# Summing the first layer's modulation on VectorE, and spreading the key lengths from a 128x8 tile

## The chip, the cores and the metric

The kernel runs on one core of one Trainium2 chip. The metric is device time in microseconds; runs of the kernel before are given as a median of three. It is one program with five instruction streams (TensorE for products, VectorE and ScalarE for elementwise work, POOL and SP for issuing transfers), each strictly in the order in which it is written, tied together by semaphores.

## The reference, cut to what matters

The model is a hybrid layer (a recurrent branch with eight heads and a dilated attention, then a mixture of experts) and behind it two further layers, each steered by a modulation vector. Two places matter here. The modulation of both later layers depends only on a conditioning vector `c` and can be computed at any time before its layer:

```
c_act = silu(c)                              # 1 x 1024
for l in range(2):
    mod = c_act @ w_ada[l] + b_ada[l]        # 1024 x 6144 weights (24 MB) for 6144 numbers
    sh_m, sc_m, gt_m, sh_f, sc_f, gt_f = split(mod, 6)
```

The keys of the recurrent branch are divided by their length in each head of 64 channels:

```
kk = heads(k * k_k)
kk = kk / maximum(sqrt(sum(kk * kk, axis=-1)), 1e-12)
wkv = scan(S = S * w + (S @ -kk) (kk * a)^T + v k^T, y = S @ r), both directions, added
```

There are 512 tokens, 1024 channels, and 8 heads of 64 channels in the recurrent branch.

## The kernel before, in words

**Stages.** A front (to 143 us) normalizes x and computes the columns of the recurrent branch. The recurrence follows (143 to 641 us), then the dilated attention, the mixture of experts, and the two later layers. The change touches the front and the recurrence; in the last layer's modulation it renames buffers.

**The recurrence** works on one pair of heads at a time, channels of both heads on the 128 partitions, 512 tokens on the free axis: four rounds, `pr` 0 to 3. Both directions `d` of the scan are done side by side. A round has a *preparation*, steps i = 5 to 28 (8 to 28 in round 0, whose first steps stand in the front), and a *row loop* of 8 chunks. `recurrence_order` (line 655) is one list of steps that all engines walk through, each doing its own part of a step. In each preparation step TensorE does 16 products of 64x64x64 (32 passes) for d = 0 and again for d = 1 (`rw_prep`, line 938) into bank 4 and bank 5, and another engine evicts each bank: ScalarE for steps 5 to 7 (line 1506), VectorE for the others (line 1994). Steps 8 to 12 make masked products (`MASKS`; step 12 gives two tiles, Dt and Lt), step 13 makes R0 from Dt on VectorE, and steps 14 to 28 are the chain `PRODS` (line 416): Dt2, D2, R0a, D4, R1a, R1b, R1c, QT, GT, Ha, Hb, KV, Hc, U1, W1T. Each of them needs the eviction of an earlier one, mostly the one ahead of it; step 14 waits for R0. There is a single bank for each direction, so an eviction also frees the bank for the next step.

**Woven work.** Between the steps stand other things, so that TensorE has something to do while a bank is evicted: in 19 of 24 steps one bank of a large product of the next stages (`rw_gemm`, line 1020), whose weights are split by ScalarE into halfH and by VectorE into halfL when a new tile begins (`split_to`, lines 1421 and 1833); the norming of the round before (`rw_norming`, VectorE); sums, scales, gains and rotations of the attention's heads (VectorE), and turns of them (TensorE into bank 6, ScalarE out of it); and the two pieces that the change is about.

**The modulation before.** `ada()` in `recurrence_order` (line 673) spreads 54 steps `("ada", g, k)` over the rounds: 9, 18, 18 and 9. In a step with k < 8 TensorE multiplies a tile of 128x1024 weights by one column of `cact` (`rw_ada`, line 1044): four products of 256 columns that write one row each. POOL loads these tiles, 48 of 512 KB, into two buffers `ada0` and `ada1`; the one for step n is issued when TensorE has done step n - 2. At k = 7 ScalarE copies the four rows to `arow`, and at k = 8 TensorE turns them (two products) and VectorE copies them to `mods`. The last layer is done otherwise, beside the feed-forward product of the layer ahead of it: VectorE multiplies a 128x1024 tile by the column and adds it to `m_acc`, transposes in blocks of 32 and reduces after eight tiles, and TensorE adds the four parts up at the end (`modulation`, lines 1066 and 2611).

**The key lengths before.** `rw_kk`: VectorE multiplies by k_k and squares; TensorE multiplies the squares by a block matrix of ones, so that each length stands on all 64 partitions of its head (128x512, line 915); ScalarE takes the root (line 1477); VectorE takes the maximum with 1e-12, the reciprocal of 128x512 and the product (line 1929). The four steps stand in four successive preparation steps of the round before (i = 5 to 8, in round 0 8 to 11), and for round 0 in the front.

**The end of the recurrence.** After the last woven tile (in step 28 of round 3) SP issues the transfers of the queries and keys for the attention (`sync_program`, line 2828). The bonus of each round (`rw_bonus`, lines 968 and 2019) stands between its preparation and its loop: VectorE forms rk2 when both W1T are evicted, TensorE multiplies it by one column.

## Time and profile before

| | |
|---|---|
| median of 3 runs | 3043.69 us (3041.87 to 3046.1) |
| the profiled execution | 3046.71 us, span 3044.8 us |
| TensorE busy | 2824.5 us, 93% |
| VectorE busy | 1586.8 us, 52% |
| ScalarE busy | 898.4 us, 30% |
| POOL busy | 109.2 us, 4% |
| chain that ended last | TensorE 78%, VectorE 12%, ScalarE 5%, DMA 2% |

The span is what the profile covers; the device time has some two microseconds around it. A matmul's end is modelled, so that two rows of TensorE may overlap: the distance of their starts is what a thing costs. An fp32 product appears as two instructions (passes). "Idle before" is the idle time of the engine ahead of an instruction, with what ended it.

### The profile page before, as it was taken

What the parts mean: (1) busy time and instruction counts of PE and PEld (TensorE: products, weight loads), DVE (VectorE), ACT (ScalarE), POOL (GpSimd) and SP (SyncE); (2) the same over time, 40 slices, a digit from 0 to 9 for tenths busy, and PEclk for the clock granted to TensorE, in tenths of its full rate; (3) what the DMA queues carried; (4) which work ended last, traced back from release to release, by engine and by line L of the source; (5) the groups of instructions that cost most, each with busy time, mean ns of one, the idle gap of its engine ahead of it and who ended that gap; (6) DMA issues with size and microseconds to landing.
All of it is one profiled execution on the core that took longest, in us unless ns stands there. A gap on an engine that the chain in (4) does not pass through costs nothing.

```text
span 3044.8 us, 47336 instructions
## 1 busy us (share of the span) xinstructions
PE 2824.5 (93%) x20508; PEld 2037.3 (67%) x20508; DVE 1586.8 (52%) x2926; ACT 898.4 (30%) x1449; POOL 109.2 (4%) x187
## 2 busy tenths in 40 slices
PE   7999999989979999989988999999999889999999
PEld 5777777866723333338666677888786656878887
DVE  4656565655543333345665456666456664554343
ACT  5323222225300100022333533223323335333131
POOL 0000000000000000000000000000000000000000
PEclk9999999999989999999998999999999989999999
DMA  4224233251399999953242334564232333323322
GB/s 146 84 75 136 85 112 119 71 188 74 104 393 427 427 426 427 427 224 93 66 97 70 131 98 151 188 198 151 83 88 70 103 71 107 102 80 93 101 94 83
DMA packets 148822, 476.87 MB, mean 157 GB/s; under 512 B 12816, under 2 KB 40064, under 8 KB 136192
## 3 DMA queue, kind: packets, MB, share of 16 engines
q1 hardware_dynamic: 114400, 367.62, 33.3%
q0 software_dynamic: 24128, 87.81, 8.8%
q10 hardware_dynamic: 10080, 18.35, 2.1%
q8 instruction: 163, 2.67, 0.4%
q14 instruction: 51, 0.42, 0.1%
HBM read 452.23 MB, written 21.51 MB: 156 GB/s over the span
## 4 chain that ended last, share of the span: by engine, by line
PE 78%; DVE 12%; ACT 5%; DMA 2%; issue 2%; POOL 0%; DVEq 0%; ACTq 0%; SPq 0%; POOLq 0%
PE psum L156 75%; PE psum L159 3%; DVE halfL L165 2%; DVE sc__234 L195 2%; DVE m L192 1%; ACT halfH L162 1%; DVE X L165 1%; DMA kT<-qk_rows 1%; DVE a20S L180 1%; DVE a21S L180 1%; DVE n_ht L168 1%; ACT a1S L162 1%; DVE slot L165 0%; DVE slot L186 0%; ACT a21S L162 0%
## 5 line engine op out<-in xcount | busy, mean ns | idle before, releaser
L165 DVE TENSOR_TENSOR halfL<-ring,halfH 128x1024 fp32r<-128x1024 f32 x302 | 368.2, 1221 | 605.2 <-ACT halfH L162 604.4
L162 ACT ACTIVATE halfH<-ring 128x1024 fp32r<-128x1024 f32 x302 | 317.1, 1053 | 747.9 <-PE psum L156 739.4
L156 PE MATMUL psum<-hH,halfH 128*128 128x512 f32 x1200 | 492.0, 410 | 9.0 <-DVE hL L165 5.3
L156 PE MATMUL psum<-hL,halfH 128*128 128x512 f32 x1200 | 476.3, 397 | 0.0
L156 PE MATMUL psum<-hH,halfL 128*128 128x512 f32 x1200 | 475.6, 396 | 0.0
L156 PEld LDWEIGHTS psum<-hH,halfH 128*128 128x128 f32 x1200 | 230.5, 192 | 90.8 <-issue 35.1
L156 PEld LDWEIGHTS psum<-hH,halfL 128*128 128x128 f32 x1200 | 230.4, 192 | 50.6
L156 PEld LDWEIGHTS psum<-hL,halfH 128*128 128x128 f32 x1200 | 231.2, 193 | 44.4 <-issue 0.2
L156 PE MATMUL psum<-halfH,hH 128*128 128x512 f32 (+2 forms) x576 | 225.8, 392 | 25.8 <-DVE hL L165 12.2
L156 PE MATMUL psum<-wslot,XT 128*64 128x512 f32 x1024 | 247.3, 606 | 0.8 <-DVE XT L165 0.8
L156 PE MATMUL psum<-halfH,hL 128*128 128x512 f32 (+2 forms) x576 | 214.8, 373 | 0.0
L156 PE MATMUL psum<-halfL,hH 128*128 128x512 f32 (+2 forms) x576 | 214.7, 373 | 0.0
L165 DVE TENSOR_TENSOR X<-X,psum 128x512 f32<-128x512 f32 x136 | 93.2, 687 | 215.8 <-PE psum L156 212.6
L156 PEld LDWEIGHTS psum<-halfH,hH 128*128 128x128 f32 x576 | 115.0, 200 | 56.3 <-issue 29.5
L156 PEld LDWEIGHTS psum<-wslot,XT 128*64 128x64 f32 x1024 | 64.3, 137 | 126.6 <-issue 125.4
L156 PEld LDWEIGHTS psum<-slot,slot 64*64 64x64 f32 x4096 | 124.6, 135 | 24.9 <-issue 18.1
L156 PE MATMUL psum<-halfH,aH 128*128 128x512 f32 x352 | 136.9, 389 | 0.0
L156 PE MATMUL psum<-halfL,aH 128*128 128x512 f32 x352 | 136.9, 389 | 0.0
L156 PE MATMUL psum<-halfH,aL 128*128 128x512 f32 x352 | 136.9, 389 | 0.0
L156 PE MATMUL psum<-slot,slot 64*64 64x64 f32 x4096 | 133.3, 220 | 3.9 <-DVE slot L165 1.9
L156 PEld LDWEIGHTS psum<-halfH,hL 128*128 128x128 f32 x576 | 115.1, 200 | 17.8
L156 PEld LDWEIGHTS psum<-halfL,hH 128*128 128x128 f32 x576 | 115.6, 201 | 14.8
(456 smaller groups left out, 4140.7 us busy)
## 6 DMA issues: line engine op xcount, KB each, us to landing
wslot<-in_w_gate SPq DMA_DIRECT2D x32, 2048.0 KB, 18.4
wslot<-in_w_up SPq DMA_DIRECT2D x32, 2048.0 KB, 18.9
wslot<-in_w_down SPq DMA_DIRECT2D x32, 2048.0 KB, 19.5
ring<-in_w_in SPq DMA_DIRECT2D x120, 512.0 KB, 3.7
ring<-in_w_gu SPq DMA_DIRECT2D x88, 512.0 KB, 3.5
ada<-in_w_ada POOLq DMA_DIRECT2D x48, 512.0 KB, 4.2
m_in<-in_w_ada POOLq DMA_DIRECT2D x48, 512.0 KB, 4.8
ring<-in_w_down SPq DMA_DIRECT2D x44, 512.0 KB, 3.9
```

Of the source, the lines that this page charges most:

```text
L156: return self.e.matmul(*a, **k)
L159: return self.e.transpose(*a, **k)
L162: return self.e.activation(*a, **k)
L165: return self.e.tensor_tensor(*a, **k)
L168: return self.e.tensor_scalar(*a, **k)
L180: return self.e.tensor_tensor_reduce(*a, **k)
L192: return self.e.max(*a, **k)
L195: return self.e.match_replace(*a, **k)
```

## The change

1. **Modulation of the first later layer.** The `ada` steps of TensorE and ScalarE, `arow` and the 48 tiles of 128x1024 go. VectorE does what it did for the last layer, on 96 tiles of 128x512: one at each preparation step (two at steps 16, 20 and 24 of round 0), none in the loops. After eight tiles it transposes and reduces. Both layers share one function on VectorE, POOL and TensorE, with widths 512 and 1024. TensorE's closing products stand in the loop of round 3, chunk 2, and VectorE's copy to `mods` at chunk 4. POOL issues 96 transfers of 256 KB.
2. **Key lengths.** TensorE sums into 128x8 (a token in each partition, tile and head in the columns), ScalarE's root and VectorE's maximum and reciprocal work on 128x8, and TensorE spreads the result over the head's 64 partitions with eight products against the identity (a fifth step, `spread`), from whose bank VectorE multiplies.
3. **Evictions.** QT, KV, U1 and W1T are evicted by ScalarE (`BY_ACT`) instead of VectorE.

```diff
+    BY_ACT = ("QT", "KV", "U1", "W1T")
+    m_in0, m_acc0, m_turn0 = [rk(f"m_in0{i}", 512) for i in range(2)], rk("m_acc0", 512), rk("m_turn0", 512)
+    MODULATION = [(m_in0, m_acc0, m_turn0, 512), (m_in1, m_acc1, m_turn1, 1024)]
...
-                 (2, 3): early("kds") + [("U", 2), ("shift", 0)] + early("Kt"),
+                 (2, 3): [("kk", 0, "spread")] + early("kds") + [("U", 2), ("shift", 0)] + early("Kt"),
...
-                if pr < 3 and i < i0 + 4:
-                    yield "kk", pr + 1, ("squares", "sums", "root", "inverse")[i - i0]
+                if pr < 3 and i < i0 + 5:
+                    yield "kk", pr + 1, ("squares", "sums", "root", "inverse", "spread")[i - i0]
...
-                for _ in range(2 if i in ((6, 7) if pr else (8, 9, 10, 11, 12)) else 1):
-                    yield from ada()
+                for _ in range(2 if not pr and i in (16, 20, 24) else 1):
+                    yield "ada",
...
+                if pr == 3 and s in (2, 4):
+                    yield ("mods", "mods_out")[s // 2 - 1],
...
# TensorE, rw_kk
-                pe.matmul(bank(Y_BANK), K("blk"), SL[0]["t1"], start=True, stop=True).then_inc(*up("rw_pe", "kk_sum", pr))
+                for t in range(4):
+                    i = pe.matmul(bank(Y_BANK)[:, 2 * t:2 * t + 2], SL[0]["t1"][:, t * 128:(t + 1) * 128],
+                                  K("blk")[:, 0:128:64], start=True, stop=True)
+                i.then_inc(*up("rw_pe", "kk_sum", pr))
                 free[Y_BANK] = [("kk_sqrt", pr)]
+            if x == "spread":
+                clear(Y_BANK)
+                pe.wait_ge(*at("kk_inverse", pr))
+                for t in range(4):
+                    for h in range(2):
+                        i = pe.matmul(bank(Y_BANK)[HP[h], t * 128:(t + 1) * 128],
+                                      kk_n[:, t, h:h + 1].to_broadcast([128, 64]), ident, start=True, stop=True)
+                i.then_inc(*up("rw_pe", "kk_spread", pr))
+                free[Y_BANK] = [("kk_normed", pr)]
...
# ScalarE, rw_prep
+            elif i >= 14 and PRODS[i - 14][0] in BY_ACT:
+                name = PRODS[i - 14][0]
                 ac.wait_ge(*at("pe", pr, d, name))
                 ac.activation(piece(d, name), bank(CHAIN_BANKS[d][i % 2]),
                               COPY).then_inc(*up(f"rw_act{d}", "ev", pr, d, name))
...
# VectorE
+        def modulation(L):
+            D = "side_dve"
+            m_in, acc, m_turn, w = MODULATION[L]
+            b = w // 32
+            for n in range(8 * 6144 // w):
+                g, k = n // 8, n % 8
+                ve.wait_ge(*at("m_in", L, n))
+                ve.wait_ge(*now(D))
+                if k == 0:
+                    ve.tensor_scalar(acc, m_in[n % 2], cact[:, 0:1], None, M).then_inc(*up(D, "m_used", L, n))
+                else:
+                    ve.scalar_tensor_tensor(out=acc, in0=m_in[n % 2], scalar=cact[:, k:k + 1], in1=acc, op0=M,
+                                            op1=AD).then_inc(*up(D, "m_used", L, n))
+                if k == 7:
+                    ve.wait_ge(*now(D))
+                    ve.transpose(m_turn, acc).then_inc(*up(D))
+                    ve.wait_ge(*now(D))
+                    ve.tensor_reduce(m_sum.rearrange("p c x -> p (c x)")[:, b * g:b * g + b],
+                                     m_turn.rearrange("p (b r) -> p b r", r=32), AX,
+                                     AD).then_inc(*up(D, *(("m_sum", L) if b * (g + 1) == 192 else ())))
+                yield
...
                 ve.wait_ge(*at("kk_sqrt", pr))
-                ve.tensor_scalar(t2, t2, 1e-12, None, MX).then_inc(*up(R_))
+                ve.tensor_scalar(kk_n, kk_n, 1e-12, None, MX).then_inc(*up(R_))
                 ve.wait_ge(*now(R_))
-                ve.reciprocal(t2, t2).then_inc(*up(R_))
-                ve.wait_ge(*now(R_))
-                ve.tensor_tensor(kk, kk, t2, M).then_inc(*up(R_))
+                ve.reciprocal(kk_n, kk_n).then_inc(*up(R_, "kk_inverse", pr))
+            if x == "spread":
+                ve.wait_ge(*at("kk_spread", pr))
+                ve.tensor_tensor(kk, kk, bank(Y_BANK), M).then_inc(*up(R_, "kk_normed", pr))
...
                 name, _, _, add, _ = PRODS[i - 14]
+                if name in BY_ACT:
+                    return
...
                 else:
                     ve.wait_ge(*now(D))
+                    ve.wait_ge(*at("ev", pr, d, "U1"))
...
# POOL
+            if n >= 2:
+                po.wait_ge(*at("m_used", L, n - 2))
+            po.dma_start(m_in[n % 2], T["w_ada_2"][L, k * 128:(k + 1) * 128,
+                                                   g * w:(g + 1) * w]).then_inc(*landed(f"m_in{n % 2}", "m_in", L, n))
+
+        for n in range(96):
+            modulation(0, n)
```

## Rows read from the trace of the kernel before

**Rows 1.** Busy time by stretch (start:end, length, busy us and instructions of each engine, clock, DMA).
```profile
143.20:212.60 69.40, 67.80 (x1352) 54.50 (x1351) 45.41 (x72) 12.29 (x20) 4.23 (x8) 1.00 0.28 88
...
263.00:359.00 96.00, 91.72 (x1854) 74.93 (x1851) 52.59 (x85) 22.47 (x40) 8.44 (x16) 1.00 0.42 133
...
411.00:506.00 95.00, 91.22 (x1779) 71.42 (x1776) 56.47 (x92) 22.38 (x37) 8.44 (x16) 1.00 0.40 128
...
561.00:641.40 80.40, 79.03 (x1622) 65.00 (x1621) 43.29 (x75) 11.26 (x20) 3.50 (x7) 1.00 0.20 65
...
641.40:661.20 19.80, 13.42 (x375) 12.52 (x373) 9.61 (x44) 1.29 (x2) 3.45 (x6) 0.98 0.89 330
```

**Rows 2.** The chain that ended last: start, length, what.
```profile
641.39 19.78 DMA kT<-qk_rows
```

**Rows 3.** Waits of TensorE from 143 to 641 us (total, times, longest).
```profile
PE psum L156 <- DMA ada<-in_w_ada: 2.8, 2, 2.6
...
PE psum L156 <- DVE slot L165: 2.5, 3, 1.0
...
PE psum L156 <- DVE Mrb L165: 2.2, 2, 1.1
```

**Rows 4.** Timeline of TensorE in round 2 (start, us, instructions).
```profile
463.11 2.08 PE L156 MATMUL psum<-slot,slot 64*64 64x64 f32 x64
...
465.12 0.61 PE L156 MATMUL psum<-ada,cact 128*1 128x256 f32 x8
...
465.66 2.08 PE L156 MATMUL psum<-slot,slot 64*64 64x64 f32 x64
```

**Rows 5.** Groups of TensorE from 60 to 680 us.
```profile
L156 PE MATMUL psum<-slot,con 128*128 128x512 f32 x8 | 4.3, 618 | 0.0
...
L156 PE MATMUL psum<-con,arow 128*128 128x4 f32 x24 | 3.4, 249 | 0.7 <-ACT arow L162 0.7
...
L156 PE MATMUL psum<-a1PT,Zv 128*64 128x128 f32 x16 | 1.1, 279 | 0.0
```

**Rows 6.** Groups of VectorE, 60 to 680 us, and of the last layer's m_acc.
```profile
L183 DVE COPY slot<-psum 128x512 f32<-128x512 f32 x48 | 33.0, 691 | 22.6 <-PE psum L156 22.1
...
L171 DVE SCALAR_TENSOR_TENSOR US<-U,colb,US 128x512 f32<-128x512 f32 x24 | 18.0, 752 | 0.9
...
L186 DVE RECIPROCAL slot<-slot 128x512 f32<-128x512 f32 x4 | 13.4, 3353 | 0.1
...
L177 DVE TENSOR_REDUCE mean<-US 128x8 f32<-128x512 f32 x4 | 2.7, 677 | 0.0
...
L171 DVE SCALAR_TENSOR_TENSOR m_acc<-m_in,cact,m_acc x34: 1277/1280/1284, 1900.3 to 2102.0; 128x1024 f32<-128x1024 f32 x34
...
L159 DVE STREAM_TRANSPOSE m_turn<-m_acc x5: 1245/1246/1246, 1930.7 to 2103.3; 128x1024 f32<-128x1024 f32 x5
```

**Rows 7.** Timeline of VectorE in round 2, step 12.
```profile
440.96 2.48 DVE L165 TENSOR_TENSOR slot<-psum,con 128x512 f32<-128x512 f32 x4 [1.40 <-PE psum L156]
```

**Rows 8.** Busy time from step 14 to step 20 of round 2.
```profile
446.20:470.80 24.60, 24.60 (x524) 19.93 (x522) 20.08 (x35) 6.11 (x12) 2.11 (x4) 1.00 0.35 110
```

**Rows 9.** Timeline at the end of preparation 0, and busy time around 210 us.
```profile
209.29 1.21 DVE L165 TENSOR_TENSOR halfL<-ring,halfH 128x1024 fp32r<-128x1024 f32 x1
...
210.42 0.69 DVE L165 TENSOR_TENSOR slot<-US,slot 128x512 f32<-128x512 f32 x1
...
211.25 1.10 PE L156 MATMUL psum<-colb,slot 64*64 64x1 f32 x32 [0.60 <-DVE slot L165]
...
210.00:220.00 10.00, 8.88 (x65) 6.14 (x63) 1.65 (x6) 2.66 (x3) 0.00 (x0) 0.83 0.28 80
```

**Rows 10.** DMA issues: count, KB each, median us to landing.
```profile
ada<-in_w_ada POOLq DMA_DIRECT2D x48, 512.0 KB, 4.2
...
m_in<-in_w_ada POOLq DMA_DIRECT2D x48, 512.0 KB, 4.8
...
bias<-in_relb POOLq DMA_DIRECT2D x16, 256.0 KB, 3.1
```

More of the change, by code:

```diff
@@ L275, in program @@
     t_pi = small("t_pi", 4, dt=I32)
-    arow = small("arow", 256)
+    m_sum = small("m_sum", 48, 4)
     g8 = small("g8", 5)
@@ L397, in program @@
     ends = [rk(f"ends{d}", 8) for d in range(2)]
+    kk_n = rk("kk_n", 4, 2)
     st = [rk(f"st{d}", 2, 64) for d in range(2)]
@@ L400, in program @@
     SA = [rk(f"SA{d}", 64) for d in range(2)]
-    ada_in = [rk(f"ada{i}", 1024) for i in range(2)]
+    m_in0, m_acc0, m_turn0 = [rk(f"m_in0{i}", 512) for i in range(2)], rk("m_acc0", 512), rk("m_turn0", 512)
     stage = [rk(f"stage{i}", 512) for i in range(2)]
@@ L671, in more @@
                     sums.append(x[1:])
-        def ada():
-            pr, c = divmod(next(calls), 27)
-            groups = (1, 2, 2, 1)[pr]
-            if (c + 1) * groups // 3 > c * groups // 3:
-                n = next(n_ada)
-                yield "ada", n // 9, n % 9
         def event(bank_free):
@@ L725, in recurrence_order @@
                 yield x
-        assert not events and not sums and next(n_ada) == 54
+        assert not events and not sums
     BETWEEN = {**{1 + i: ("norming", 3, i) for i in range(9)}, 12: ("gated", 3), 14: ("turned", 3)}
@@ L1361, in tensor_program @@
         handlers = {"rkv": rkv_tile, "kk": rw_kk, "lora": rw_lora, "values": rw_values, "prep": rw_prep, "bonus": rw_bonus,
-                    "loop": rw_loop, "gated": rw_gated, "turned": rw_turned, "ada": rw_ada, "gemm": rw_gemm,
-                    "turn": a1_turn}
+                    "loop": rw_loop, "gated": rw_gated, "turned": rw_turned, "gemm": rw_gemm,
+                    "turn": a1_turn, "mods": lambda: modulation(0)}
         for step, *args in recurrence_order():
@@ L1396, in tensor_program @@
             if L:
-                modulation()
+                modulation(1)
             norm(f"n3{L}", n3_xn)
@@ L1573, in a1_turn @@
             turned_last[0] = (("a1", who, ci), "turn", j)
-        def rw_ada(g, k):
-            if k == 7:
-                ac.wait_ge(*at("ada", 8 * g + 7))
-                for j in range(4):
-                    i = ac.activation(arow[32 * j:32 * j + 1, :], bank(ADA_BANK)[32 * j:32 * j + 1, 0:256], COPY)
-                    i.then_inc(*up("ada_act", *(("ada_row", g) if j == 3 else ())))
         sq_free = [None, None]
@@ L2131, in a1_rope_, with rw_ada, rw_mods_out @@
                 also(H_, "a1", who, ci, "rope")
-        def rw_ada(g, k):
-            if k == 8:
-                ve.wait_ge(*at("ada_turned", g))
-                m = mods[:, 8 * g:8 * g + 8].rearrange("p (n c) -> p c n", c=2)
-                ve.tensor_copy(m, bank(ADA_BANK)[:, 0:8].rearrange("p (c n) -> p c n",
-                                                                       n=4)).then_inc(*up("ada_dve", "mods", g))
+        first_layer = modulation(0)
+        def rw_ada():
+            next(first_layer)
+        def rw_mods_out():
+            ve.wait_ge(*at("mods", 0))
+            ve.tensor_copy(mods, bank(ADA_BANK)[:, 0:48]).then_inc(*up("side_dve", "mods_out"))
         H_ = "hd_dve"
@@ L2509, in modulated @@
             D = "side_dve"
-            for g in range(6):
-                ve.wait_ge(*at("mods", g))
             if L:
@@ L2514, in modulated @@
                 ve.wait_ge(*at("mod_out", 0))
-                ve.wait_ge(*at("mods1"))
+                ve.wait_ge(*at("mods", 1))
+            ve.wait_ge(*now(D))
             ve.tensor_tensor(mod, bank(GEMM_BANKS[0])[:, 0:48] if L else mods, col(f"bada{L}", 0, 48), AD).then_inc(*up(D, "mod", L))
@@ L2609, in chosen @@
             ve.wait_ge(*now(D))
[L2611 to L2630 removed]
         def ffn(L):
             tag, D = f"f{L}", "ev_dve"
[L2634 removed]
+            beside_ffn[0] = None if L else modulation(1)
             for part, (ups, nk, down) in enumerate(G_ffn[L]):
@@ L2739, in pool_program, with modulation @@
         also("gqk", "gqk_in")
-        for n in range(48):
-            part, k = n // 8, n % 8
+        def modulation(L, n):
+            m_in, _, _, w = MODULATION[L]
+            g, k = n // 8, n % 8
             if n >= 2:
-                po.wait_ge(*at("ada", n - 2))
-            po.dma_start(ada_in[n % 2], T["w_ada_2"][0, k * 128:(k + 1) * 128,
-                                                     part * 1024:(part + 1) * 1024]).then_inc(*landed(f"ada{n % 2}",
-                                                                                                      "ada_in", n))
+                po.wait_ge(*at("m_used", L, n - 2))
[3 more added lines that the diff above has]
+            modulation(0, n)
         po.wait_ge(*at("tile", LAST_WOVEN))
@@ L2819, in pool_program @@
             for n in range(48 * (L == 0)):
[L2820 to L2825 removed]
+                modulation(1, n)
     def sync_program(sp):
```

81 lines of the change are left out of this document (17 added, 64 removed).

## The prediction

> **What bounds the kernel now.** I read the busy time in 40 slices first: TensorE is at 9 tenths nearly everywhere. The change touches the recurrence, which runs from 143 to 641 us, so I asked for busy time in stretches there. It has four rounds (one for each pair of heads, 0 to 3), each a preparation of 24 steps and a row loop. In the preparations TensorE works 67.8 of 69.4, 91.7 of 96, 91.2 of 95 and 79.0 of 80.4 us, VectorE 45.4, 52.6, 56.5 and 43.3 us, ScalarE under a quarter [rows 1]. So TensorE's instruction stream sets the pace, and VectorE has a third to spare on the mean. The chain that ended last shows how this stage ends: the last woven tile is done at 641.4, then a 19.8 us transfer of the keys runs [rows 2], beside which the last row loop keeps TensorE busy for only 13.4 us [rows 1]. Whatever brings that last tile forward brings all later work forward; what sits in the last loop is covered.
>
> The waits of TensorE in the recurrence are short: 2.8 us for the modulation's weights, 2.5 for slots and 2.2 for a mask product Mrb, both from VectorE [rows 3]. Each 1.1 us wait for Mrb follows the 3.35 us reciprocal [rows 6].
>
> **What is taken off TensorE.** A modulation step costs 0.61 us of matmuls, 0.54 from its start to the next step's (465.12 to 465.66) [rows 4]: 48 x 0.54 = 25.9 us. The turn of a row costs 3.4/6 = 0.57 [rows 5], 0.5 by start-to-start; five of six lie ahead of the last tile: 2.5 us. The wait for the weights goes: 2.8. The reciprocal on 128x512 becomes one on 128x8, so the two Mrb waits go (2.2) and a like one of 1.0 in preparation 0, the longest of the slot waits [rows 3]. Sum 34.4 us. On ScalarE 24 small copies go, which bound nothing but one short wait.
>
> **What is added to TensorE.** Key sums: one 128x512 product (4.3/4 = 1.1 us [rows 5]) becomes four with 2 columns; by the row turn (two products with few columns, 0.57) that is 1.1 us, no change. The spread is 8 products of 128 columns, 16 passes. By 16 passes of 128x128 from a1PT at 1.1 us [rows 5] it costs 1.1 us; by the loaded 128x128 turn (four instructions 0.57 us) 2.3. I take 1.1, nearest in shape: 3 x 1.1 = 3.3 us (bounds 3.3 to 7). The fourth, ahead of 143 us, stands against the reciprocal that VectorE, packed there, no longer does: nought, +-1. The 16 closing products of the modulation and their copy lie in the last loop: 13.4 + 2 us is under 19.8, free; without that cover they would be 2 us.
>
> **What is added to VectorE.** 84 multiply-adds and 12 multiplies on 128x512: the sibling on 128x1024 takes 1.28 us [rows 6], a 128x512 one of that kind 0.75. Twelve transposes (half of 1.25, 0.7 with the fixed part) and twelve reduces (0.68). That is 63 + 5 + 8.4 + 8.2 = 85 us; off go 32 copies at 0.69 (22 us) and three reciprocals of 3.35 [rows 6]. Net +53 us on the 198 of the four preparations [rows 1], which get shorter. Two independent operations of this size start 0.6 us apart though each lasts 0.69, as four in 2.48 show [rows 7]; so I take 0.7 for a multiply-add between others. The Trainium skill (VectorE: DVE Perf Modes, "The DRAIN you can't avoid") lets the next operation start only when the pipe is empty; by this rule each of the 96 would take the whole 0.75, VectorE would have 5 us more to do, and the sum would be some 2 us smaller.
> The mean still fits; single steps don't. VectorE is in order: a step's two evictions, 0.6 us apart, then its side work, then the next evictions. TensorE may start the next step once the first eviction is there; so side work up to about 3.6 us is hidden between two full steps of 3.6, and 2 us where one has no woven product (463.11 to 465.12 [rows 4]). I went through the steps with these numbers, adding 0.7 for each step, 2.2 where a group of eight ends:
> - Groups end at steps 12, 20 and 28 in preparations 1 to 3. Step 12 is the worst place: four masked evictions (2.48 [rows 7]), then 2.2 us, and only then R0, for which TensorE waits at step 14. In preparation 2, counted from the start of step 12: evictions 1.2 to 3.6, sums to 5.8, first R0 there at 6.55; TensorE, with 2.0 of products and two woven ones of 1.6, is there at 5.15. New wait 2.7 (a split comes on top, and 0.9 is waited already), 1.4 and 0.8 us in preparations 1, 2, 3, and 0.65 in 0, where the spread stands in between.
> - Preparation 2, steps 14 to 20: VectorE is busy 20.1 of 24.6 us [rows 8]. Plus 7 x 0.7 + 1.5 makes 26.5, against TensorE's 24.6 - 2.7 = 21.9. This stretch goes over to VectorE. With the slack spent first, waits of 2.5 us are left; preparation 1: 0.3.
> - Steps 21, 25, 27, 28 now evict on ScalarE, which has the time; that alone is nought, and adds no wait where the eviction is all it does. Where such a step also splits a tile, the split queues behind both evictions on ScalarE and VectorE waits for it. Worst at step 28 of preparation 0: split, group end and rk2 in a row. Today the split ends at 210.4 and rk2 starts there, with TensorE 0.6 us late [rows 9]; then the split ends at 211.6, the group at 213.7 and rk2 at 214.4: +3.2. Preparation 1 the same way +1.6, preparation 2 +0.2, and 0.4 at a step 21.
> - In step 9 of preparations 1 and 2 the turn wants the bank of the spread, which VectorE must read first: 0.9 each.
> - Doubled modulation steps in preparation 0 want a third transfer early: 0.5.
> New waits together: 0.65 + 3.2 + 0.5 (0), 2.7 + 0.3 + 1.6 + 0.9 (1), 1.4 + 2.5 + 0.4 + 0.2 + 0.9 (2), 0.8 (3) = 16 us.
>
> **The sum.** 34.4 - 3.3 - 16 = 15 us saved. The profiled execution took 3046.7 us with a span of 3044.8, 3 us above the median of 3043.7. So 3031.7 for such an execution and **3028.5** for the median. Elsewhere nothing changes but buffer names, and the last layer's modulation keeps its widths.
>
> **Transfers.** The weights come as 96 times 256 KB where 48 times 512 KB took 4.2 us to land [rows 10]; 256 KB of another POOL transfer took 3.1. With two buffers VectorE can take one every (3.1 to 4.2 + 0.5 + 0.8)/2 = 2.2 to 2.75 us, under a step of 3.6: hidden. POOL issues 48 more, at 0.53 us (16 in 8.44 [rows 1]); nothing else is queued there before 641 us.
>
> **Rivals.**
> - **A, all of it pays** (chance 0.2): the waits are swallowed, because ScalarE's evictions break the lag and the groups' ends fall beside slack. Then up to 31 us: 3013 to 3021. For it: VectorE has a third idle [rows 1]; against it step 12, where nothing is between.
> - **B, VectorE becomes the bound in all heavy stretches** (0.2): my slack of 3.6 us per step is too kind, and every step with norming or head work overruns as the stretch of preparation 2 does. New waits of 26 to 34 us then leave 5 us of gain or a loss of 3: 3038 to 3046. For it: the stretch above [rows 8], and that any lag falls on both chains.
> - **C, slower** (0.06): the weights come late. The wait for them now stands on VectorE ahead of both chains' evictions. The same kind of transfer took 4.8 us beside VectorE's sums in the later layer [rows 10]. At 7 us a multiply-add gets its tile only every 4.2 us: 96 x 4.2 = 400 us against the 341 of preparations, +59 and, with the gains used up, 3100; it turns to a loss from about 6 us a transfer. The Trainium skill (SBUF — State Buffer, "Two separate sides") says that VectorE in its two-port mode locks out GpSimd, which must write the descriptors of its own transfers, so that these starve. By this rule the added work would slow just these transfers. The trace half agrees: 4.8 beside those sums against 4.2.
> - **D, the granted clock** (0.04 on its own): around 210 us, after the wait and the one-column bonus products, the mean clock is 0.83 over 10 us [rows 9], that is 3.4 us at 1.2 GHz, 1.7 lost. The new waits could bring one such fall in each preparation, 4 x 1.7 = 7 us off my gain: 3035. The Trainium skill (TensorE: Matmul & The Clock Gate, "HAM oscillation") says that idle gaps send the array back to half clock; by this rule the wait at the end of preparation 0 costs more than itself.
> - **The change does nothing** because TensorE isn't the bound: excluded by its 97% in the preparations [rows 1]; no chance of its own.
>
> **How the numbers follow.** My forecast, 8 to 22 us saved, has 0.5. The range takes A's near part and B's near half, and D: 3015 to 3040. About 0.2% (6 us) is what a measurement of this kernel can tell from no change. Faster by more: the forecast, A, D and half of B: 0.84. The same: the other half of B, 0.10. Slower: C, 0.06.
>
> **What would show it.** TensorE's matmuls from the weights gone, a row of 96 multiply-add groups near 0.75 us on VectorE, its busy time in the preparations near 59, 66, 70 and 56 us; the key transfer starting near 626 instead of 641.4; TensorE's waits for slots on VectorE, 2.5 us now, near 15, the longest at the first bonus (about 3.8) and ahead of each step 14. I am wrong if the key transfer moves by less than 6 us, if VectorE waits for the weights by more than 5 us in total, or if matmuls outside the recurrence change.

## The result, and the profile after

| | kernel before | changed kernel |
|---|---|---|
| median, first comparison | 3044.89 us (4 runs) | 3027.38 us (3025.74 to 3029.69, 4 runs) |
| ratio | | 0.9947, 95% 0.9932 to 0.9962 |
| median, repeated beside the experiments | 3040.85 us (16 runs) | 3025.79 us (10 runs) |
| ratio | | 0.9953, 95% 0.9936 to 0.9969 |
| profiled execution | 3046.71 us, span 3044.8 | 3025.74 us, span 3023.8 |

By the medians the change saves 17.5 us in the first comparison and 15.1 in the larger one, where 15 were forecast. The chain of waits of the changed kernel has the key transfer at 629.5 us; it was at 641.4 [rows 2].

```profile
629.47 19.91 DMA kT<-qk_rows
```

The modulation's and the key lengths' groups, from the groups by shape of VectorE and TensorE up to 660 us (busy us, mean ns, idle before). The multiply-add takes 744 ns and a spread 1.1 us for its 16 passes (64 passes, 4.4 us), as assumed.

```profile
L171 DVE SCALAR_TENSOR_TENSOR m_acc<-m_in,cact,m_acc 128x512 f32<-128x512 f32 x84 | 62.5, 744 | 15.0 <-DMA m_in<-in_w_ada 14.5
...
L159 DVE STREAM_TRANSPOSE m_turn<-m_acc 128x512 f32<-128x512 f32 x12 | 8.5, 712 | 0.4
L177 DVE TENSOR_REDUCE m_sum<-m_turn 128x16 f32<-128x512 f32 x12 | 8.2, 686 | 0.4
```
```profile
L156 PE MATMUL psum<-con,kk_n 128*64 128x128 f32 x64 | 4.4, 279 | 0.0
L156 PE MATMUL psum<-con,slot 128*128 128x2 f32 x32 | 4.0, 247 | 0.0
```

Busy time by stretch, the four preparations (they begin and end earlier than in [rows 1]; columns as there). VectorE works 54.8, 61.8, 65.5 and 55.8 us; forecast were 59, 66, 70 and 56 (more on these under the costs of single operations).

```profile
143.20:216.50 73.30, 64.81 (x1301) 54.28 (x1298) 54.78 (x95) 15.17 (x24) 12.36 (x23) 1.00 0.40 121
266.90:356.40 89.50, 83.49 (x1729) 74.50 (x1726) 61.84 (x104) 23.43 (x40) 12.90 (x24) 1.00 0.40 123
408.30:498.00 89.70, 83.65 (x1628) 71.16 (x1624) 65.48 (x112) 22.84 (x36) 12.36 (x23) 0.98 0.39 119
553.10:629.50 76.40, 73.42 (x1531) 63.17 (x1526) 55.82 (x96) 14.43 (x24) 11.10 (x21) 1.00 0.32 97
```

The waits of TensorE from 143 to 629 us (total, times, longest). The waits for the old weights and for Mrb [rows 3] are gone; those for slots have grown from 2.5 to 15.7 us.

```profile
PE psum L156 <- DVE slot L165: 15.7, 12, 3.7
PE psum L156 <- ACT slot L162: 2.6, 7, 0.5
PE psum L156 <- DVE slot L183: 2.5, 2, 1.7
...
PE psum L159 <- DVE slot L165: 1.6, 2, 0.8
```

TensorE's timeline has them where the forecast put them: the first bonus, and step 14 of preparations 1, 2 and 3.

```profile
215.16 1.09 PE L156 MATMUL psum<-colb,slot 64*64 64x1 f32 x32 [3.70 <-DVE slot L165]
...
299.10 1.11 PE L156 MATMUL psum<-slot,slot 64*64 64x64 f32 x31 [2.55 <-DVE slot L165]
...
437.15 1.05 PE L156 MATMUL psum<-slot,slot 64*64 64x64 f32 x29 [1.53 <-DVE slot L165]
...
576.12 1.09 PE L156 MATMUL psum<-slot,slot 64*64 64x64 f32 x30 [1.05 <-DVE slot L165]
```

What was not forecast is on the same chain of waits: it runs through transfers of the new weights, three times in preparation 0 and once in preparation 2 (start, length from issue to use). VectorE's timeline shows two of its waits for them in preparation 0; the last line is SP's issue of a tile of the products' weights (512 KB) just ahead of the transfer at 176.27.

```profile
176.27 5.36 DMA m_in<-in_w_ada
...
182.70 2.95 DMA m_in<-in_w_ada
...
196.91 4.80 DMA m_in<-in_w_ada
...
466.79 5.53 DMA m_in<-in_w_ada
```
```profile
181.65 1.61 DVE L171 SCALAR_TENSOR_TENSOR m_acc<-m_in,cact,m_acc 128x512 f32<-128x512 f32 x2 [1.60 <-DMA m_in<-in_w_ada]
...
185.67 0.75 DVE L171 SCALAR_TENSOR_TENSOR m_acc<-m_in,cact,m_acc 128x512 f32<-128x512 f32 x1 [2.33 <-DMA m_in<-in_w_ada]
```
```profile
175.34 0.37 SPq L198 DMA_DIRECT2D ring<-in_w_in  x1
```

By the bonus products the key transfer's 11.9 us come together so: preparation 0 loses 3.9 us (211.25 [rows 9] to 215.16), then round 1 gains 6.6, round 2 gains 5.3 and round 3 gains 4.0 up to the transfer. The recurrence itself began 0.8 us earlier (its first eviction of Mrk at 144.2 instead of 145.0), so that preparation 0, counted from there, loses 4.7 us. The rest of the kernel is the same: from the key transfer to the end it takes 2317 us at full clock in both traces (2403.4 and 2394.3 us as they ran). The two profiled spans are 21 us apart, then, but 9 of these are clock outside the recurrence.

### The profile page after: what moved, and what is told of

It is laid out like the page before. It is cut to its first block, busy times and chain, and to the rows that moved or that the text cites. A ratio compares the mean times of both kernels' runs of the same rounds, so it can differ in the third digit from the quotient of the medians.

```text
span 3023.8 us, 46989 instructions
## 1 busy us (share of the span) xinstructions
PE 2796.5 (92%) x20220; PEld 2036.4 (67%) x20220; DVE 1625.0 (54%) x3008; ACT 905.8 (30%) x1457; POOL 135.5 (4%) x235
## 4 chain that ended last, share of the span: by engine, by line
PE 77%; DVE 13%; ACT 5%; DMA 3%; issue 2%; POOL 0%; SPq 0%; DVEq 0%; ACTq 0%; POOLq 0%
PE psum L156 74%; PE psum L159 3%; DVE halfL L165 2%; DVE sc__237 L195 2%; DVE m L192 1%; ACT halfH L162 1%; DVE X L165 1%; DMA kT<-qk_rows 1%; DVE slot L165 1%; DVE a21S L180 1%; DVE a20S L180 1%; DMA m_in<-in_w_ada 1%; ACT a1S L162 1%; DVE n_ht L168 1%; DVE m_acc L171 0%
```

## How the experiments are read

Differences of 3 us are smaller than the scatter of single executions (the kernel before: 3028 to 3049 us), and much of that scatter is TensorE's granted clock. Each execution is listed with its span and mean clock, so two means over all executions can be told apart: the time **lost to the clock**, span x (1 - clock), and the span **at full clock**, span x clock. The columns of the table are differences to the executions of the kernel before that ran beside that kernel, with one standard error. The same ones stand behind keys_alone, mod_alone, all_on_vector and third_buffer (26 executions), behind the repeated changed kernel, late_end, late_third and no_modulation (16), and behind mod_and_act, third_again and placed (15); long_reciprocal has its own (17). The last column is from the one profiled execution: from the first eviction of Mrk (the start of the recurrence) to the key transfer, in brackets without what the lower clock cost there (summed over stretches of 5 us). The kernel before has 496.4 (493.0) there, and loses 90 to 93 us to the clock in all. How far single traces agree, the changed kernel shows: its first trace has 485.3 (480.2), 3.4 more than its second. The first has a wait of 1.9 us at 475 us that the second lacks, and a fall of the clock behind it that cost 1.7. Differences of the last column under 2 us are not told apart.

| kernel | executions | ratio (95%) | span | at full clock | lost to the clock | recurrence |
|---|---|---|---|---|---|---|
| changed, repeated | 10 | 0.9953 (0.9936 to 0.9969) | -15.2 ±2.1 | -13.9 ±1.0 | -1.3 ±1.8 | 481.9 (478.5) |
| keys_alone | 12 | 1.0 (0.9989 to 1.001) | -0.7 ±1.4 | -0.2 ±0.6 | -0.5 ±1.4 | 494.3 (490.9) |
| mod_alone | 12 | 1.0007 (0.9993 to 1.002) | +2.4 ±1.8 | -6.5 ±1.0 | +9.0 ±1.8 | 496.7 (481.2) |
| all_on_vector | 9 | 0.9968 (0.9955 to 0.9981) | -10.0 ±1.5 | -9.8 ±0.8 | -0.2 ±1.5 | 489.0 (480.4) |
| mod_and_act | 11 | 0.9983 (0.997 to 0.9996) | -4.3 ±1.7 | -12.8 ±1.2 | +8.5 ±1.7 | 489.5 (475.8) |
| long_reciprocal | 12 | 0.997 (0.9958 to 0.9981) | -8.8 ±1.5 | -8.9 ±0.9 | +0.1 ±1.5 | 491.7 (481.5) |
| third_buffer | 6 | 0.9954 (0.9938 to 0.9969) | -14.7 ±1.4 | -12.5 ±0.9 | -2.2 ±1.5 | 478.6 (475.2) |
| third_again | 5 | 0.9921 (0.9908 to 0.9935) | -22.1 ±1.8 | -15.0 ±1.6 | -7.1 ±1.5 | 478.7 (475.2) |
| late_end | 7 | 0.9942 (0.9921 to 0.9963) | -18.1 ±2.2 | -17.2 ±1.2 | -0.9 ±2.1 | 481.2 (476.0) |
| late_third | 6 | 0.9934 (0.9913 to 0.9954) | -19.7 ±2.2 | -19.0 ±1.1 | -0.7 ±2.0 | 477.7 (472.4) |
| placed | 5 | 0.9931 (0.9917 to 0.9944) | -18.2 ±1.5 | -14.2 ±1.4 | -4.0 ±1.5 | 480.9 (475.8) |
| no_modulation | 6 | 0.9899 (0.9875 to 0.9923) | -33.1 ±2.8 | -30.5 ±1.0 | -2.5 ±2.9 | 464.4 (462.7) |

## Which part carries the gain

**The changed kernel, repeated** (`changed_again`, no edit).

> The changed kernel once more, unchanged, for more executions beside the other kernels of this call. 3027 us by the first four runs; a ratio to the kernel before of 0.994 to 0.996. Theory G (the granted clock matters: what a kernel gains is partly given back in falls of the clock): its time lost to the lower clock (span times one minus the mean clock) is within 2 us of that of the kernel before, so that the gain is all in TensorE's own stream.

Measured: 0.9953, and -1.3 ±1.8 us lost to the clock. For the whole change nothing is given back to the clock, as theory G has it for this kernel, and rival D, 7 us, is out.

**Key lengths alone** (`keys_alone`): the kernel before with the diff's `rw_kk` parts and the step `spread`.

> The kernel before with only the key lengths changed (part 2). Theory of the prediction: three reciprocals' waits of TensorE go (3.2 us), three spreads come (3.3 us) and two turns wait for the bank of the spread (up to 1.8 us): key transfer at 641.4 to 643.5, time 3044 to 3047, no difference that can be measured. Rival: the 3.35 us reciprocals held up more than the waits that show on TensorE; then the key transfer starts 4 us or more earlier, below 637.5, and the time is 3040 or less.

Measured: ratio 1.000. The trace's key transfer came at 635.3, which looks like the rival's case, but 4.0 us of that were there before the recurrence began (its first Mrk at 141.0, not 145.0; 1.7 of them are a higher clock in the front, the rest is unexplained) and 2.1 us are left. The executions' medians are equal (3040.6 and 3040.5): no difference, as the theory said.

**Modulation alone** (`mod_alone`): the changed kernel with the old `rw_kk` and this line.

```diff
-    BY_ACT = ("QT", "KV", "U1", "W1T")
+    BY_ACT = ()
```

> The changed kernel with the key lengths as before and all evictions on VectorE: of the three parts only the modulation is changed. Theory of the prediction: it carries the whole gain. The reciprocals come back beside more work of VectorE (3 to 6 us more waits), the spreads and the waits for their bank go (5 us): key transfer at 628 to 634, time 3026 to 3033. Rival B (VectorE is the bound): its 32 us more than in the changed kernel show for the most part, key transfer at 641 or later, no gain over the kernel before.

Measured: 1.0007, no gain. My expectation failed outright: the modulation was to carry everything. Rival B's numbers came out (key transfer at 641.0, no gain), but its cause is at most half of it. At full clock this kernel is 6.5 us shorter than the kernel before, and it loses 9.0 us more to the clock; in the trace 15.5 us of the recurrence are lost so, against 3.4. Its timeline of TensorE shows the wait for Mrb, 1.1 us before [rows 3], at 2.7 us, and busy time by stretch the clock behind it and behind the wait of step 14:

```profile
287.49 1.81 PE L156 MATMUL psum<-R,slot 64*64 64x64 f32 x38 [2.69 <-DVE Mrb L165]
...
304.77 1.50 PE L156 MATMUL psum<-slot,slot 64*64 64x64 f32 x29 [2.54 <-DVE slot L165]
```
```profile
288.00:292.00 4.00, 4.00 (x58) 3.68 (x55) 2.66 (x5) 0.00 (x0) 0.54 (x1) 0.57 0.46 150
305.00:309.00 4.00, 4.00 (x91) 4.00 (x88) 2.14 (x5) 0.00 (x0) 0.54 (x1) 0.57 0.36 123
```

A mean of 0.57 is nearly all at 1.2 instead of 2.4 GHz. VectorE's timeline of the same place shows why the wait has grown: multiply-add, two evictions, maximum, reciprocal, product and the next multiply-add stand in one row ahead of the eviction of Mrb.

```profile
280.45 1.28 DVE L165 TENSOR_TENSOR slot<-psum,con 128x512 f32<-128x512 f32 x2
281.64 0.42 DVE L168 TENSOR_SCALAR slot<-slot 128x512 f32<-128x512 f32 x1
282.10 3.35 DVE L186 RECIPROCAL slot<-slot 128x512 f32<-128x512 f32 x1
285.48 0.69 DVE L165 TENSOR_TENSOR slot<-slot,slot 128x512 f32<-128x512 f32 x1
286.09 0.75 DVE L171 SCALAR_TENSOR_TENSOR m_acc<-m_in,cact,m_acc 128x512 f32<-128x512 f32 x1
286.75 1.28 DVE L165 TENSOR_TENSOR Mrb<-psum,con 128x512 f32<-128x512 f32 x2
```

**Without the evictions on ScalarE** (`all_on_vector`): the changed kernel with `BY_ACT = ()` alone.

> The changed kernel with QT, KV, U1 and W1T evicted by VectorE again: VectorE gets 32 copies (22 us) back in the four preparations. Theory of the prediction: TensorE's stream sets the pace and moving these evictions is worth next to nothing in itself, since they stand in steps 21, 25, 27 and 28, where VectorE has slack; in preparation 0 the split of step 28 no longer queues on ScalarE (1 us less at the first bonus), a few tenths are lost elsewhere. Key transfer at 629.5 +- 3 us, time within 4 us of the changed kernel's 3027.4. Rival B (VectorE has become the bound): half or more of the 22 us shows, the key transfer starts at 640 or later and the time is 3038 or more.

Measured: 3029.8 us, the key transfer at 631.4: within the theory's bounds, and rival B is out. Against modulation alone it shows what the new key lengths are worth beside the sums: 12.4 us of span (3.3 at full clock, 9.2 of the clock), of which nothing shows when they are done alone. Against the changed kernel part 3 is worth 5.2 ±2.6 us (4.1 ±1.3 at full clock) and not nought. Without it the first bonus waits 1.0 us less (2.72 instead of 3.70), but the later three wait 2.6, 1.6 and 2.0 us instead of 1.4, 0.4 and 0.9. `mod_alone` against `mod_and_act`, which comes next, gives 6.7 ±2.5 us for part 3 (6.3 ±1.6 at full clock).

**Modulation and evictions** (`mod_and_act`): the changed kernel with the old `rw_kk`.

> The changed kernel with the key lengths as before: parts 1 and 3 without part 2, the last corner of the comparison. If the parts' effects on TensorE's stream at full clock add up, its span at full clock (span times mean clock) lies 3 to 4 us above the changed kernel's. Theory G (the long reciprocals, beside the sums, make waits of over 2 us on TensorE, and the granted clock falls after them): it loses 5 to 9 us more to the lower clock than the kernel before, so that in all it takes 8 to 13 us more than the changed kernel and gains only 2 to 7 us on the kernel before. Rival (the reciprocals cost only what they hold up): no more lost to the clock, 3 to 4 us more than the changed kernel in all.

Measured: 0.9983, within all that G says: 8.5 ±1.7 us more lost to the clock than the kernel before (5 to 9 expected), a gain of 4.3. At full clock it is only 1.1 ±1.6 us behind the changed kernel, less than the 3 to 4 expected. So beside the sums, the new key lengths are worth 11 to 12 us, and 9 to 10 of them come by the clock. Two pairs of kernels show it, with and without part 3.

**The reciprocal by itself** (`long_reciprocal`): the changed kernel with a dead one behind the short one.

```diff
                 ve.reciprocal(kk_n, kk_n).then_inc(*up(R_, "kk_inverse", pr))
+                if pr:
+                    ve.wait_ge(*now(R_))
+                    ve.reciprocal(SL[1]["t1"], US[:, 4 + pr, :]).then_inc(*up(R_))
```

> The changed kernel with one reciprocal on 128x512 (3.35 us), whose result nobody reads, behind the short one in preparations 0, 1 and 2: three instructions more on VectorE, 10 us, and nothing on TensorE. Theory G: it brings back the three waits of TensorE that the kernels with the old key lengths show (3.1 us near 158, 2.7 and 2.3 us for Mrb), which cost 5 to 8 us at full clock, and with them the falls of the clock: 6 to 9 us more lost to the lower clock than in the kernel before of the same call. Time 11 to 16 us above the changed kernel's, ratio to the kernel before 0.998 to 1.001. Rival (the clock was lost by something else of the old key lengths, such as the missing spreads or the long root on ScalarE): the waits come back, the loss to the clock stays within 2 us of the kernel before's, and the ratio is 0.9965 to 0.998. Rival S (VectorE has slack at these steps): no waits, ratio 0.995 to 0.996.

Measured: 0.997 and, at full clock, 5.0 us more than the changed kernel: the waits of 2.6 and 2.2 us are back. But its mean loss to the clock is that of the kernel before (+0.1 ±1.5). The rival's numbers came out, not G's. In the profiled execution the clock does fall behind these waits:

```profile
286.25 1.11 PE L159 MATMUL psum<-con,Zst 128*128 128x128 f32 x4 [2.61 <-DVE slot L165]
```
```profile
286.00:292.00 6.00, 5.75 (x71) 5.11 (x72) 2.53 (x5) 1.28 (x2) 0.54 (x1) 0.50 0.53 173
```

Over twelve executions, though, it is not the 9 us of the other two. In all the three long reciprocals cost 6.4 ±2.6 us of span, not the 11 or more of G. The old key lengths have more that this kernel does not: a maximum and a product of 128x512 on either side of the reciprocal, the long root, no spreads, and a wait of 3.1 us at 158 us with a fall of the clock behind it, where this kernel waits 1.6 us and keeps its clock. Which of these costs the rest was not tried and stays open.

## Where the gain goes

**The bound** (`no_modulation`).

```diff
-                for _ in range(2 if not pr and i in (16, 20, 24) else 1):
-                    yield "ada",
...
-        for n in range(96):
-            modulation(0, n)
...
+        ve.memset(mods, 0.0).then_inc(*up("side_dve"))
```

> The changed kernel with the first later layer's modulation left out altogether (no weights, no multiply-adds, no closing products; the modulation is set to zero): the bound of what the sums beside the products cost. Theory of the prediction: of the 16 us of new waits all but the splits on ScalarE (2 us) and the waits for the spread's bank (1.6 us) go, so the key transfer comes 10 to 13 us earlier than in the changed kernel, 3013 to 3017 us. Theory G: falls of the clock in the recurrence go too, 3 to 5 us more of time. If the difference is under 5 us, VectorE's sums are hidden nearly everywhere and my list of waits is wrong.

Measured: 3009.1 us, the key transfer 17.3 us earlier. So the sums beside the products still cost 17.8 ±2.9 us (16.6 at full clock), more than the 10 to 13 expected, and TensorE's freed stream with part 2 and 3 is worth 30.5 ±1.0 at full clock: the forecast's 34.4 - 3.3 = 31.1, less the 3.6 for the splits and the bank of the spread, was 27.5. Theory G's further 3 to 5 us of clock did not show (1.2 ±3.0). The wait at the first bonus falls to 1.6 us: the 0.6 of before [rows 9] and 1.0 for the split that now stands behind ScalarE's evictions.

**Three buffers for the weights** (`third_buffer`, `third_again`).

```diff
-    m_in0, m_acc0, m_turn0 = [rk(f"m_in0{i}", 512) for i in range(2)], rk("m_acc0", 512), rk("m_turn0", 512)
+    m_in0, m_acc0 = [rk(f"m_in0{i}", 512) for i in range(3)], rk("m_acc0", 512)
...
-            if n >= 2:
-                po.wait_ge(*at("m_used", L, n - 2))
+            if n >= len(m_in):
+                po.wait_ge(*at("m_used", L, n - len(m_in)))
```

> The changed kernel with three buffers for the 256 KB weight tiles in place of two (the transpose goes into the buffer just used instead of one of its own). VectorE's waits for the weights, 14.5 us in the changed kernel and 9 of them in preparation 0, should fall below 4 us in either case. Theory W (late weights are why preparation 0 lost 3.4 us more than predicted): TensorE gets 3 us or more back, the first bonus starts at 212 or earlier instead of 215.2 and the key transfer at 626.5 or earlier, time 3024 or less. Rival S (those waits lie in VectorE's slack, and the loss is from the split, the end of a group and rk2 in a row at step 28): the first bonus starts at 214.2 or later, key transfer within 1.5 us of 629.5, time 3026 to 3029.

> The changed kernel with three buffers for the weight tiles, once more, for more executions: preparation 0 was 3.3 us shorter in its trace, but the time was not clearly below the changed kernel's. If the third buffer is worth what preparation 0 shows, the ratio to the kernel before is 0.9935 to 0.9945; if it is worth nothing in all, 0.995 or above.

Measured: VectorE's waits for the weights fall from 14.5 to 0.2 us.

```profile
DVE m_acc L171 <- DMA m_in<-in_w_ada: 0.2, 1, 0.2
```

The trace bears out W: the first bonus comes 67.7 us after the start of the recurrence in both traces with three buffers, and 71.0 and 70.9 in those with two. It still waits the same 3.7 us, so this wait is not the weights' doing; what goes are the waits in its middle (1.7 us at 189.5 and 1.1 at 203.8).

```profile
211.99 1.09 PE L156 MATMUL psum<-colb,slot 64*64 64x1 f32 x32 [3.70 <-DVE slot L165]
```

The recurrence is 3.3 us shorter at full clock than in the repeated changed kernel, twice. The whole time doesn't settle it. The median of `third_buffer`, 3026.9 us, is rival S's and not W's 3024 or less; the ratios are 0.9954 and 0.9921, on either side of the 0.9935 to 0.9945 that the second run was to show, at full clock -12.5 ±0.9 and -15.0 ±1.6 against -13.9 ±1.0. The gain of 3 us is shown for the recurrence, and not resolved in the whole.

**The end of a group one step later** (`late_end`, and with three buffers `late_third`); `end` is the transpose and the reduce.

```diff
             for n in range(8 * 6144 // w):
                 g, k = n // 8, n % 8
+                if k == 0 and g and not L:
+                    end(g - 1)
...
-                if k == 7:
+                if k == 7 and L:
...
             if pr == 3:
+                yield "ada",
```

> The changed kernel with the end of each group of eight (transpose and reduce, 1.4 us) done one step later, ahead of the next group's first multiply: at steps 13, 21 and 5 of the next preparation instead of 12, 20 and 28. Theory of the prediction (TensorE waits where a group's end stands ahead of an eviction it needs): the waits at step 14 (2.6, 1.5, 1.1 us) and at the first bonus (3.7 us) shrink by 1.0 to 1.4 us each, the other bonus waits go; 6 to 8 us of waits less in all, key transfer 5 to 8 us earlier counted from the start of the recurrence, time 3 to 7 us below the changed kernel's. Rival B (VectorE is saturated on the mean): a moved end only moves the wait to the next step; less than 2 us of difference.

> Both edits: three buffers for the weight tiles and the group's end one step later. If the two are independent, the key transfer comes 3 us earlier for the third buffer (66.2 to 68 us from the start of the recurrence to the first bonus) and 5 to 8 us earlier for the late end: time 3017 to 3023. If both only uncover the same slack, no better than the better of the two.

Measured: 3022.9 and 3020.0 us. The named waits fall as expected: the first bonus from 3.7 to 2.2, step 14 from 2.6 to 1.1 in preparation 1, the second, third and fourth bonus to nothing. But about half comes back one step on. In the timeline of TensorE in `late_end`:

```profile
295.92 2.08 PE L156 MATMUL psum<-slot,slot 64*64 64x64 f32 x64 [1.08 <-DVE slot L165]
298.97 1.21 PE L156 MATMUL psum<-slot,slot 64*64 64x64 f32 x34 [0.96 <-DVE slot L183]
```

Its waits for slots by the two lines are 8.2 + 5.9 = 14.1 us against 14.6 + 2.6 = 17.2 in the repeated changed kernel: 3.1 less, and 3.3 ±1.4 less at full clock, where 6 to 8 were expected. Theory and rival B each have half of it. With three buffers as well (`late_third`) it is 4.4 ±2.3 us below the changed kernel measured beside it (5.1 ±1.3 at full clock): of these kernels the best that computes everything, though by the time itself hardly more than the measurement tells. In the recurrence at full clock the two edits add up rather than uncover the same slack: 3.3 and 2.5 us alone, 6.1 together.

**Steps moved away from the norming** (`placed`), on top of `late_third`.

```diff
-                for _ in range(2 if not pr and i in (16, 20, 24) else 1):
+                for _ in range({0: {16: 2, 18: 2, 20: 2, 22: 2, 24: 2, 27: 0, 28: 0}, 3: {}}.get(
+                        pr, {14: 0, 15: 0, 16: 0, 17: 0, 22: 2, 23: 2, 24: 2, 26: 2}).get(i, 1)):
                     yield "ada",
```

> The kernel with three buffers and the late end of a group, and the modulation's steps moved: in preparations 1 and 2 none at steps 14 to 17 (the norming and the first products of the chain) and two each at 22, 23, 24 and 26; in preparation 0 none at 27 and 28 and two also at 18 and 22. The same 24 in each preparation, VectorE's busy time unchanged. Theory of the prediction (TensorE waits where single steps of VectorE overrun, while the mean fits): the waits of 1.1 and 1.0 us near step 14 of preparation 1 and of 1.6, 1.2 and 1.4 us in preparation 2 mostly go (4 us or more of 6.3), the first bonus waits 1.6 us instead of 2.2; time 4 to 6 us below that of three buffers with the late end, 3013 to 3017 beside a kernel before of 3040. Rival B (the mean load sets it): the waits come back at steps 22 to 26, and the time is within 1.5 us of that kernel's.

Measured: a miss. The ratio is no better than that of `late_third` (0.9931 and 0.9934), and the recurrence at full clock is 3.4 us longer. Rival B's numbers came out. The waits of 1.2 and 1.4 us in preparation 2 went and one of 3.1 came, at step 25 (KV); those of 1.1 and 1.0 in preparation 1 and of 1.6 in preparation 2, which were to go, stayed. In preparation 1 a new one came; VectorE's timeline and TensorE's wait for it:

```profile
328.64 0.74 DVE L171 SCALAR_TENSOR_TENSOR m_acc<-m_in,cact,m_acc 128x512 f32<-128x512 f32 x1
329.42 0.71 DVE L159 STREAM_TRANSPOSE m_in<-m_acc 128x512 f32<-128x512 f32 x1
330.16 0.69 DVE L177 TENSOR_REDUCE m_sum<-m_in 128x16 f32<-128x512 f32 x1
331.60 0.48 DVE L168 TENSOR_SCALAR m_acc<-m_in,cact 128x512 f32<-128x512 f32 x1 [0.75 <-DMA m_in<-in_w_ada]
```
```profile
332.81 1.38 PE L156 MATMUL psum<-Vn,slot 64*64 64x64 f32 x40 [2.15 <-DVE slot L165]
```

I had put two tiles and the end of a group into one step (23), with the weights late again (0.8 us). A step has room for one unit beside its evictions, hardly for three. The first bonus did fall to the 1.6 us expected, and preparation 0 was no shorter (66.4 and 66.3 us): a wait of 1.0 us had come in at 177.

## Why the prediction was right, and where it was not

The forecast, 3028.5, stands 1 us from the first median, and its 15 us saved are 15.2 ±2.1 in the larger comparison. What set the pace, where TensorE would wait and what single operations cost was right. That the total fits so closely is in part luck. Here are the gains of the recurrence by my terms and by the two traces, from its start to the first bonus, then from bonus to bonus, and to the key transfer:

| | my terms | first trace | repeated |
|---|---|---|---|
| preparation 0 | -0.1 | -4.7 | -4.7 |
| round 1 | 4.1 | 6.6 | 6.6 |
| round 2 | 6.8 | 5.3 | 8.5 |
| round 3 | 4.0 | 4.0 | 4.1 |

By its steps:

- **TensorE's stream sets the pace.** Right. With the modulation out of the way the kernel is 30.5 us shorter at full clock, against 27.5 by my terms, and nothing outside the recurrence moved. The sums beside the products take 16.6 of it back, against 12.4 by my terms (16 less 3.6). Two errors of 3 and 4 us offset each other.
- **The costs of single operations.** Right within some hundredths of a microsecond: multiply-add 0.744 (0.75 assumed), transpose 0.71, reduce 0.69, spread 1.1, sums 1.0 for 1.1, and the two waits for the spread's bank 0.8 each for 0.9. VectorE's busy time came out 13 us lower in all, 238 us for 251. I had spread the 53 us evenly over the preparations, though preparation 3 has no reciprocal to lose; shared out rightly, each of the four is some 3 us lower. Neighbours overlap: a multiply-add of 0.744 us whose successor starts after 0.66 accounts for some 2 us of it, by estimate from the 21 of them in each.
- **The first bonus.** Forecast: split to 211.6, group end to 213.7, rk2 at 214.4, a wait of 3.8 us. Measured ends: 212.3, 214.4 and 215.0, the whole row 0.6 to 0.7 us late because the preparation was, and a wait of 3.70. The parts are confirmed one by one: 1.0 us from ScalarE's queue (`all_on_vector`), 1.5 from the group's end (`late_end`). The other bonuses wait 1.4 and 0.4 us, where 1.6 and 0.2 were given.
- **Step 14.** Forecast: new waits of 2.7, 1.4 and 0.8. Measured: 2.55, 1.53 and 1.05; but of the 2.55 the kernel before had 0.92 already, so that the new wait is 1.6 and the sum's 2.7 was 1.1 us too dark. The group's end is the cause: done a step later, it leaves 1.1 us of the first, and 1.0 comes back at the next step.
- **Steps 14 to 20 of preparation 2.** Forecast 2.5 us; measured 1.2 at step 20. The first trace has 1.9 more at step 25, where VectorE had stood 1.6 us for its weights; the repeated one doesn't. So the term was twice too large.
- **"Transfers: hidden" is the step that failed.** I put 0.5 us for it and named 5 us of waiting as the point at which I would be wrong; VectorE waited 14.5 us, 9 of them in preparation 0. There are two causes. One is the pace: with two buffers the third of three tiles that stand close together at a doubled step can only be fetched when the first is used: 2.3 us of waiting at 185.7, ahead of a group's end, though the tile landed in 2.95 us. The other I overlooked: the median landing was 3.1 us, as assumed, but landings went up to 6.2, and nine of the eleven waits were for tiles that took 3.7 us or more. The one issued at 176.27 took 5.4, and VectorE stood 1.6 us for it, where 3.1 would have been in time. By estimate, with each of the eleven landed in 3.1 us, 5.7 of the 14.5 us would be left. SP had issued a 512 KB tile of the products' weights 0.9 us before that one (175.34 above), and 1.3 us before the 5.5 us one at 466.79. In the repeated trace the tile at this place took 5.7. That the two transfers slow each other is likely, but no run moved one of them. Price of both causes, by three buffers: 3.3 us of TensorE's time instead of 0.5. That is most of preparation 0's loss of 4.7 us; the rest no run took apart; two waits of 0.6 and 0.8 us near 158 are part of it.
- **That the forecast was met in spite of it** is due to terms that were too dark elsewhere: round 1 gained 2.5 us more than my terms, and round 2 in the repeated trace 1.7 more. Of these 4.2 us, 1.1 are step 14, 1.3 the stretch of preparation 2, and 1.3 two short waits of the kernel before that went with the rest (0.6 at 303, 0.7 for `arow` at 358).
- **"That alone is nought"**, said of moving the evictions to ScalarE, was wrong by some 5 us. It didn't touch the sum, since the bonus waits were forecast with part 3 in place.
- **The reciprocals.** 3.2 us were set against 3.3 for the spreads, so part 2 came to nought. Alone it is nought. Beside the sums it carries 11 to 12 us, mostly by the clock, which the sum left to rival D. It added up parts that do not add up, and was right only for all three together.
- **Rivals.** A is out (15.7 us of waits for slots). B is out as a mean load: VectorE is at 69 to 75% of the preparations; as a local effect half of it is true (`late_end`, `placed`). C has the right place (late tiles on VectorE), but it had all transfers at 7 us and a price of 59 us; the median stayed at 3.1 beside the added work, and the price is 3.3. D is out for the changed kernel (-1.3 ±1.8 us lost to the clock), but it is what happens to the modulation without part 2, 9 us.

The Trainium skill (VectorE: DVE Perf Modes, "The DRAIN you can't avoid") would have each multiply-add block the pipe for its whole time. The timeline shows otherwise: the one of 0.75 us at 286.09 above is followed by the next start at 286.75, after 0.66 us. The section itself refers to instructions that are not held, which start earlier; that is the case here, and I had read the rule without it.

## What to carry to other kernels

Work that is moved to an engine with a third of its time free costs TensorE what single steps overrun, here half of the 31 us taken off it: go through the steps, find the longest row of instructions ahead of each eviction, and put no group's end, split or reciprocal of 3 us into the same row. Parts of a change that load the same step are not additive, so measure the corners, not only each part alone. Where two buffers feed an engine, a doubled step needs a third; and whether two are enough is read from the longest landings, not from the median.

## What was not expected of the hardware

**The clock can cost more than the wait.** Two kernels lose 8.5 and 9.0 us (±1.8) more to the lower clock than the kernel before, with waits of 2.3 to 3.1 us in their preparations. Yet a wait alone does not decide it. The 2.55 us wait of step 14 in preparation 1 leaves the clock at 1.00 in the changed kernel, and so it does in all five traces that have it and no long reciprocal. The same wait of 2.54 us has 0.57 behind it in `mod_alone` (above), where another one of 2.7 us came 17 us earlier, and a fall follows it in each of the three traces that have such an earlier one. The row of the changed kernel, by stretch:

```profile
299.00:303.00 4.00, 3.90 (x128) 3.91 (x128) 3.39 (x7) 0.00 (x0) 0.54 (x1) 1.00 0.49 156
```

Over the recurrences of all fourteen traces it reads so: each of the fourteen waits longer than 2.6 us has a fall behind it, the six of 3.7 us at the first bonus among them (0.66 over 215 to 220 us in the changed kernel). Of the shorter ones, 2.58 us for the weights in the kernel before and those of 2.2 to 2.3 us for evictions away from a bonus have none, while the 1.9 us at 475 in the changed kernel's first trace has one. Ahead of a bonus and its one-column products it takes less: 1.6 us in `no_modulation` (0.73 over 6 us), and in the kernel before 0.6 (0.83 over 10 us [rows 9]), where `keys_alone`, with the same 0.6, has no fall. The Trainium skill (TensorE: Matmul & The Clock Gate, "HAM oscillation") says that idle gaps send the array to half clock. The traces agree for the longest ones; they show that a fall doesn't follow each wait of 2.5 us, and that it can come behind a shorter one. Why `long_reciprocal`, with nearly the waits of `mod_alone`, does not lose the 9 us over its executions is open.
